# The second layer's modulation, multiplied and summed on VectorE instead of TensorE, in the weight stream of a one-core block kernel

## The reference, cut to what matters

```python
c_act, cc_act = silu(c), silu(c_ctx)                 # two vectors of 2048
for i in range(2):
    mod_l = c_act  @ ada_w[i] + ada_b[i]             # ada_w[i]: 2048 x 6144
    mod_c = cc_act @ ada_w[i] + ada_b[i]
    sh, sc, gt = split(mod, 3)                       # for latents and for context
    h = rms_norm(x, norm_gain[i]) * (1 + sc) + sh
    y = retention(h)  if i == 0 else  attention(h)   # 8 retention heads / 16 query heads
    x = x + gt * y
```

## Time and profile before

| | us |
|---|---|
| median of 3 runs | 3257.87 |
| lowest and highest | 3254.32, 3258.62 |
| the profiled execution, its own time | 3256.36 |
| its span, first to last instruction | 3255.0 |
| TensorE busy (share) | 3185.1 (98%) |
| VectorE busy (share) | 1751.4 (54%) |
| ScalarE busy (share) | 1295.1 (40%) |
| mean granted TensorE clock, share of full | 0.995 |

### The profile page before, as it was taken

The page is one execution under the profiler, slowest core; times in us unless marked ns, Lnnn a source line. Parts: engine busy times, 40 slices in busy tenths (PEclk is TensorE's granted clock), DMA queues, the critical chain, the costliest instruction groups (busy, mean ns, idle before and its releaser), DMA issues.

```text
span 3255.0 us, 48439 instructions
## 1 busy us (share of the span) xinstructions
PE 3185.1 (98%) x20536; PEld 2764.2 (85%) x20536; DVE 1751.4 (54%) x2608; ACT 1295.1 (40%) x1878; POOL 0.2 (0%) x4
## 2 busy tenths in 40 slices
PE   8999999999999999999998999999999999999998
PEld 6677777877778787777876889988999999999998
DVE  5543544435444353444436667778776665555555
ACT  4443232232232323223233645556554444444443
POOL 0000000000000000000000000000000000000000
PEclk9999999999999999999999999999999999999999
DMA  9854433233332333323234424444655545556564
GB/s 369 313 199 175 171 113 130 97 110 130 117 129 97 111 122 117 136 97 123 101 113 181 136 98 156 143 143 154 204 171 177 182 163 169 180 193 195 195 194 149
DMA packets 153927, 508.98 MB, mean 156 GB/s; under 512 B 15344, under 2 KB 35952, under 8 KB 152944
## 3 DMA queue, kind: packets, MB, share of 16 engines
q1 hardware_dynamic: 149328, 493.03, 44.1%
q10 hardware_dynamic: 4384, 12.85, 1.0%
HBM read 501.62 MB, written 4.19 MB: 155 GB/s over the span
## 4 chain that ended last, share of the span: by engine, by line
PE 89%; DVE 5%; ACT 3%; DMA 2%; issue 1%; SPq 1%; ACTq 0%; DVEq 0%
PE bank L594 28%; PE bank L596 27%; PE bank L595 27%; PE bank L656 3%; DMA raw<-stream 1%; DVE w_lo L1722 1%; ACT w_hi L1123 1%; PE bank L874 1%; ACT a_s L1431 1%; SPq L567 0%; PE bank L820 0%; PE bank L672 0%; DVE a_s L2133 0%; DVE a_numbers L2143 0%; DMA raw_h<-stream 0%
## 5 line engine op out<-in xcount | busy, mean ns | idle before, releaser
L594 PE MATMUL bank<-h_hi,w_hi 128*128 128x256 f32 (+1 forms) x4032 | 1259.5, 312 | 11.6 <-DVE w_lo L1722 6.0
L596 PE MATMUL bank<-h_hi,w_lo 128*128 128x256 f32 (+1 forms) x4032 | 1240.0, 308 | 0.0
L595 PE MATMUL bank<-h_lo,w_hi 128*128 128x256 f32 (+1 forms) x4032 | 1239.3, 307 | 0.0
L1722 DVE TENSOR_TENSOR w_lo<-raw,w_hi 128x1024 fp32r<-128x1024 f32 x729 | 882.1, 1223 | 584.0 <-ACT w_hi L1123 580.0
L1123 ACT ACTIVATE w_hi<-raw 128x1024 fp32r<-128x1024 f32 x729 | 761.9, 1058 | 914.1 <-PE bank L596 567.4
L594 PEld LDWEIGHTS bank<-h_hi,w_hi 128*128 128x128 f32 x4032 | 759.5, 188 | 84.2 <-issue 38.8
L595 PEld LDWEIGHTS bank<-h_lo,w_hi 128*128 128x128 f32 x4032 | 759.8, 188 | 44.8 <-issue 3.1
L596 PEld LDWEIGHTS bank<-h_hi,w_lo 128*128 128x128 f32 x4032 | 759.3, 188 | 43.7
L594 PE MATMUL bank<-w_hi,h_hi 128*128 128x512 f32 x704 | 286.7, 407 | 13.3 <-DVE w_lo L1722 6.5
L596 PE MATMUL bank<-w_hi,h_lo 128*128 128x512 f32 x704 | 276.5, 393 | 0.0
L595 PE MATMUL bank<-w_lo,h_hi 128*128 128x512 f32 x704 | 275.9, 392 | 0.0
(11 more groups left out here) (265 smaller groups left out, 2869.3 us busy)
## 6 DMA issues: line engine op xcount, KB each, us to landing
raw<-stream SPq DMA_DIRECT2D x904, 512.0 KB, 4.2
raw_h<-stream SPq DMA_DIRECT2D x32, 512.0 KB, 10.4
res<-tokens_in ACTq DMA_DIRECT2D x4, 1024.0 KB, 8.6
vg<-mem_in ACTq DMA_DIRECT2D x4, 512.0 KB, 8.8
h_hi<-mem_kv ACTq DMA_DIRECT2D x2, 1024.0 KB, 10.3
out<-res SPq DMA_DIRECT2D x4, 512.0 KB, 3.0
mem_kv<-qk ACTq DMA_DIRECT2D x1, 1024.0 KB, 7.9
mem_kv<-vg ACTq DMA_DIRECT2D x1, 1024.0 KB, 7.3
```

The lines of the kernel that those rows point to most:

```text
L594: pe.matmul(out, sh, mh, start=start, stop=False, **checks)
L595: pe.matmul(out, sh, ml, start=False, stop=False, **checks)
L596: return pe.matmul(out, sl, mh, start=False, stop=stop, **checks)
L1722: dve.tensor_tensor(in_quarters(m.low(raw)[:, :]), m.raw[SLOT[raw]], in_quarters(m.w_hi[slot][:, :]).bitcast(F32), ALU.subtract).then_inc( ...
```

## The change

The 96 chunks of layer 1 leave TensorE. They stay in the stream, 512 KB each, in another layout: a chunk `("mod", q, t)` now holds, for 2 x 128 of the 6144 outputs (on the partitions), the weights of a quarter `q` of the 2048 inputs. VectorE multiplies it with the condition, which has been laid across all partitions, and sums along the row: for each chunk two output tiles times two conditions, so four instructions `tensor_tensor_reduce` over 512 elements, each with a second small one behind it that writes the sum. The first quarter starts from the bias, later ones from the sum so far. This is done in VectorE's `weights_to`, just ahead of the low part of the next weight in the stream. `MODS` puts the chunks at places of heads 1 to 7: 16 in each of heads 1 to 6, less two places that are left empty at each change of the quarter, and 6 at the tiles of head 7.

The condition goes through memory: ScalarE's queue writes it once (16 KB) and SyncE's queue loads a quarter of it, the same 4 KB to all 128 partitions (512 KB), at four points of the stream (`RELOAD`), behind the last use of the quarter before. `modulated` multiplies the gain in one instruction in the last head. A raw buffer with a `mod` chunk is free when VectorE has read it. Layer 0's modulation is as it was.

```diff
-for _h in range(1, RET_HEADS - 1):
-    BESIDE[_h] = modulation_beside(places_of_head((1,) * 8, (1,) * 8), [(1, n) for n in range(3 * _h - 3, 3 * _h)])
-
-BESIDE[RET_HEADS - 1] = modulation_beside(
-    places_of_head((1,) * 6 + (0,), ()) + [(("o",), 2), (("t", 7), 0)] + [(("r", n), 2) for n in range(KT // 2)],
-    [(1, n) for n in range(18, 24)])
+for _h in range(1, RET_HEADS):
+    BESIDE[_h] = {}
+
+MOD_QUARTERS, MOD_PAIRS = 4, MOD_TILES // 2
+MOD_K = P // MOD_QUARTERS
+def modulation_on_vector():
+    steps = [(q, t) for q in range(MOD_QUARTERS) for t in range(MOD_PAIRS)]
+    out, gap = {}, 0
+    for h in range(1, RET_HEADS):
+        last = h == RET_HEADS - 1
+        places = [("t", i) for i in range(6 if last else 8)]
+        if not last:
+            places += [("v", 0), ("v", 1)] + [("r", n) for n in (0, 1, 2, 3, 5, 7)]
+        for place in places:
+            if not steps:
+                break
+            if steps[0][1] == 0 and steps[0][0] and gap < 2:
+                gap += 1
+                continue
+            gap = 0
+            out[(h, *place)] = steps.pop(0)
+    return out
...
+RELOAD = {WHERE["ada", 0, MOD_TILES // 2 - 1][3] + 12: 0}
+for _q in range(1, MOD_QUARTERS):
+    RELOAD[FIRST["mod", _q - 1, MOD_PAIRS - 1] + SLOTS] = _q
...
 # SyncE, for each chunk c of the stream
+        if c in RELOAD:
+            q = RELOAD[c]
+            if q == 0:
+                sp.wait_ge(s.load["c_out"], 16)
+                sp.wait_ge(*s["ada_turned"].at(*GROUPS[-1]))
+            else:
+                sp.wait_ge(*s["modded"].at(q - 1, MOD_PAIRS - 1))
+            rows = d["c_rows"][MOD_K * q:MOD_K * (q + 1), :].rearrange("a b -> (a b)").unsqueeze(0)
+            sp.dma_start(m.c_rows[:, :, :, :].rearrange("p a b c -> p (a b c)"), rows.broadcast_to([P, MOD_K * 2 * KT])
+                         ).then_inc(s.load["c_rows"], 16)
+        if before is not None and MOD_USE[before]:
+            sp.wait_ge(*s["modded"].at(*STREAM[before][0][1:]))
...
 # VectorE
     def weights_to(c, count=SLOTS):
         while split[0] < min(Q[c] + count, len(SPLIT)) and NEEDS[SPLIT[split[0]]] <= c:
             n, raw = split[0], SPLIT[split[0]]
             split[0] += 1
+            while mods and FIRST[mods[0]] < raw:
+                modulate(*mods.pop(0)[1:])
             dve.wait_ge(s.hi, n + 1)
...
+    def modulate(q, t):
+        c = FIRST["mod", q, t]
+        dve.wait_ge(s.raw[SLOT[c]], 16 * USE[c])
+        if t == 0:
+            dve.wait_ge(s.load["c_rows"], 16 * (q + 1))
+        if q or t:
+            dve.wait_ge(*s["modded"].now())
+        for j in range(2):
+            k = 2 * t + j
+            w = m.raw[SLOT[c]][:, 2 * j:2 * j + 2, :].rearrange("p a (b c) -> p (a b) c", c=KT)
+            for b in range(2):
+                x = m.mod[1][:, k, b:b + 1]
+                start = x if q else m.bias1[:, 1, k - KT:k - KT + 1] if KT <= k < 2 * KT else m.param("ada_b1", k, 1)
+                i = dve.tensor_tensor_reduce(out=w if b else m.products[:, j, :, :], in0=w, in1=m.c_rows[:, :, b, :], scale=1.0, scalar=start,
+                                             op0=ALU.mult, op1=ALU.add, accum_out=x)
+        i.then_inc(*s["modded"].up(q, t))
```

More of the change, by code:

```diff
@@ L161, in beside @@
             ada(layer, n, (c,))
+        if (h, *slot) in MODS:
+            q, t = MODS[(h, *slot)]
+            out.append((("mod", q, t), "ada_w", 1, MOD_K * q, 0, 2 * P * t, 0))
     beside("start", "begin")
@@ L257 @@
 RAW_USE = [b[0][0] == "ada" for b in STREAM]
-SPLIT = [c for c in range(CHUNKS) if not RAW_USE[c]]
+MOD_USE = [b[0][0] == "mod" for b in STREAM]
+SPLIT = [c for c in range(CHUNKS) if not RAW_USE[c] and not MOD_USE[c]]
 Q = [0]
-for _raw in RAW_USE:
-    Q.append(Q[-1] + (not _raw))
+for _c in range(CHUNKS):
+    Q.append(Q[-1] + (not RAW_USE[_c] and not MOD_USE[_c]))
+DONE = [_c + 1 - sum(MOD_USE[:_c + 1]) for _c in range(CHUNKS)]
 WIDEST = WHERE["mv", 1][7] // (2 * WIDE) * (2 * WIDE)
@@ L453, in __init__ @@
         self.o_rstd = sb("o_rstd", [P, T])
+        self.products = nc.alloc_sbuf_tensor_at("products", [P, 2, MOD_K, KT], BF16, offset=at[0] - 4 * T)
         self.rope0 = sb("r_rope", [P, 4, L])
@@ L562, in sync_program @@
         slot, before = SLOT[c], BEFORE[c]
-        if before is not None and RAW_USE[before]:
-            sp.wait_ge(s.mm, before + 1)
+        if c in RELOAD:
[10 more added lines that the diff above has]
+            sp.wait_ge(*s["modded"].at(*STREAM[before][0][1:]))
+        elif before is not None and RAW_USE[before]:
+            sp.wait_ge(s.mm, DONE[before])
         elif before is not None:
@@ L1129, in done @@
     def done(what, n=2):
-        act.wait_ge(s.mm, WHERE[what][n - 1] + 1)
+        act.wait_ge(s.mm, DONE[WHERE[what][n - 1]])
     def psum(*what):
@@ L1235, in scalar_program @@
                 tokens_in(n // 2 - 1)
+            if half and n == 3:
+                act.wait_ge(*s["cond_rows"].at())
+                act.dma_start(d["c_rows"], flat(m.cond_rows)).then_inc(s.load["c_out"], 16)
     for n in range(2):
@@ L1713, in vector_program @@
     split = [0]
+    mods = [("mod", q, t) for q in range(MOD_QUARTERS) for t in range(MOD_PAIRS)]
     def weights_to(c, count=SLOTS):
@@ L1728, in done @@
     def done(what, n=2):
-        dve.wait_ge(s.mm, WHERE[what][n - 1] + 1)
+        dve.wait_ge(s.mm, DONE[WHERE[what][n - 1]])
     def psum(*what):
@@ L2022, in vector_program @@
                     add_square("x1", 2 * n + j, BOTH)
-                beside(h, "r", n)
+            beside(h, "r", n)
+            if last and n == 0:
+                modulated()
     for side, cols in ((0, LAT), (1, SIDE)):
@@ L2406 @@
     stream = np.empty((CHUNKS, P, CHUNK), np.float32)
-    for c, (_, name, layer, k0, nk, n0, nn) in enumerate(STREAM):
+    for c, (what, name, layer, k0, nk, n0, nn) in enumerate(STREAM):
+        if what[0] == "mod":
+            block = w[name][layer][:, n0:n0 + 2 * P].reshape(KT, P, 2, P)[:, k0:k0 + MOD_K]
+            stream[c].reshape(P, 2, MOD_K, KT)[...] = block.transpose(3, 2, 1, 0)
+            continue
         block = w[name][layer][k0 * P:(k0 + nk) * P, n0:n0 + nn]
```

37 lines of the change are left out of this document (21 added, 16 removed).

## The result

| us | before | after |
|---|---|---|
| median (4 runs of each, on the same chip) | 3257.16 | 3171.45 |
| lowest and highest | 3254.32, 3258.62 | 3170.17, 3177.02 |
| span of the profiled execution (its own time) | 3255.0 | 3170.1 (3171.53) |

The ratio is 0.9743 (95% interval 0.973 to 0.9755): 2.6% faster. The forecast was 3171.

What follows compares the result with a forecast made beforehand. TensorE, busy for 98% of the span, was taken as the bound. Terms of 64 + 5.3 + 5.6 + 9.5 + 2.2 = 86.6 us came off 3256.4, giving 3169.8, plus 1.5 to the median: 3171 us, range 3163 to 3200.

Steps and rivals of the forecast that it cites:

- What a chunk costs TensorE in heads 1 to 6: Heads 1 to 6: 0.80 us a chunk, 10.7 us a head with the turns, 64 us (47 to 67) saved.
- The last head's output pairs: Last head: the next six output pairs go from 7.03 us each to 5.44, saving 9.5 us.
- The chain to the first pair: Last head: square root some 6 us earlier without the late DMA, so the first output pair ends 5.6 us sooner.
- now it begins with the end of the tile: Last head: tile 3's tanh starts when the tile ends, 1722.9 instead of 1727.44, and the pair ends at 1728.9.
- The two chunks behind the outputs: Last head: removing them saves nothing, since TensorE waits for the sums of squares until 1710.74 anyway.
- The start of layer 1: Start of layer 1: two low parts of 1.14 us each, made ahead of the last pair, save 2.2 us (0 to 3).
- VectorE's price: VectorE: 0.80 us an instruction with its write, 3.2 a chunk (2.4 to 5.8), 72% of a head, all hidden.
- Half rate: Rival on VectorE: a chunk costs 5.8 us, heads last 188 to 198 us, 3201 in all; 10 in 100.
- The slow load: Rival: the condition's load takes 25 us instead of 4.2, some 10 us at each of four, 3211; 4 in 100.
- The dearer instruction: Rival on VectorE: gain undone from 6.2 us a chunk on; at 2 us an instruction about 3411; 5 in 100.
- Nothing is gained: Rival: TensorE's matmul stream gets a wait at each tile in place of the chunk; 2 in 100.
- the end of the `ada` records: Sign in the profile after: TensorE's `ada` line has about half its records and ends near 340 us.

Runs made afterwards that it cites:

- b_one: The kernel before, with only one of the four matmuls of each layer-1 modulation chunk kept: 3256.64 us, ratio 0.9997.
- b_nolast: The kernel before, with head 7's 24 modulation chunks moved to heads 1 to 6, two at every tile, still on TensorE: 3240.05 us, ratio 0.995.
- a_none: The changed kernel without layer 1's modulation chunks, multiplications and condition loads, its bias standing in: 3173.16 us, ratio 0.9742 to the kernel before.
- a_nogap: The changed kernel without the two empty places at each change of quarter: 3172.08 us, ratio 0.9736 to the kernel before.
- a_twice: The changed kernel with each multiplication with its sum done twice, the extra sum unread: 3210.33 us, ratio 0.9855 to the kernel before.
- a_thrice: The changed kernel with each multiplication with its sum done three times, the extra sums unread: 3513.58 us, ratio 1.0787 to the kernel before.
- b_paired: The kernel before, with heads 1 to 6's layer-1 chunks two at a time at every second place: 3250.55 us, ratio 0.9981.

## Why the prediction was right, and where a term was off

**What a chunk costs TensorE in heads 1 to 6** held: 10.7 us a head, 0.80 a chunk by the distance of tiles. `b_one` shows that it is the break; had I priced the records (0.64) or the bare distance (0.57), I would have had 47 to 55 us instead of 64. The three stretches up to the last mean gave 69.2 of 69.3 us.

**The total** agrees better than its terms. The sum took off 86.6 us and the profiled spans differ by 84.9. These 1.7 us too many met the 1.5 us that I had added because the profiled execution before lay under its median; the one after lies 0.1 above its own. That the median came within 0.5 us is in part luck.

**The last head's output pairs** held: from 1734.51 to 1776.67 there were six pairs of 7.03 us; after, they are 5.44 apart (1666.52, 1671.96, and so on), 9.5 us for six.

**The chain to the first pair** was right in its mechanism and 1.2 us off in size. ScalarE's square root in the changed kernel, where in the kernel before a copy stood ahead of it that had waited 3.90 us for a DMA:

```profile
1643.63 0.69 ACT L1206 ACTIVATE o_rstd<-bank,eps 128x512 f32<-128x512 f32 x1 [1.97 <-PE bank L823]
```

It now waits for the mean alone. VectorE's rows of the changed kernel at the first and the last pair:

```profile
1661.08 1.66 DVE L1979 SCALAR_TENSOR_TENSOR res<-bank,mod,res 128x256 f32<-128x256 f32 x4 [0.27 <-PE bank L643]
...
1666.52 1.66 DVE L1979 SCALAR_TENSOR_TENSOR res<-bank,mod,res 128x256 f32<-128x256 f32 x4 [0.91 <-PE bank L643]
...
1699.16 1.66 DVE L2106 SCALAR_TENSOR_TENSOR res<-bank,mod,res 128x256 f32<-128x256 f32 x4 [2.38 <-PE bank L643]
...
1706.41 0.42 DVE L2127 TENSOR_TENSOR h_lo<-a_s,h_hi 128x256 fp32r<-128x256 f32 x1
```

The tanh of tile 3 starts at 1655.04 in this kernel, and the additions stand 6.04 us behind it, as forecast (6.0). But the next pair's first product comes at 1660.88, 19.3 us behind the mean, where I had 18.2 (23.77 less 5.6). The gain was 4.4. The step that was short is "now it begins with the end of the tile", where I let tile 3 take what it took before. TensorE's timeline after shows why it took longer:

```profile
1641.55 2.04 PE L823 MATMUL bank<-qk,ones_dv 128*128 128x512 f32 x2 [2.77 <-DVE qk L2046]
1642.61 1.42 PE L641 MATMUL bank<-h_hi,w_hi 128*128 128x512 f32 x1
1643.82 0.63 PE L642 MATMUL bank<-h_lo,w_hi 128*128 128x512 f32 x1
```

The mean takes 2.04 us here and 1.10 before. By stretch, the 3.3 us from the mean on, this kernel and then `b_nolast`:

```profile
1641.50:1644.80 3.30, 3.25 (x6) 2.00 (x7) 3.30 (x5) 0.85 (x2) 0.00 (x0) 0.54 0.00 0
```

```profile
1709.00:1712.30 3.30, 3.29 (x13) 2.39 (x14) 3.30 (x5) 0.82 (x2) 0.00 (x0) 1.00 0.00 0
```

Both waited the same 2.77 us for the mean. One was granted 0.54 of the clock after it, about its lower level of 1.2 GHz, the other all of it (2.4), and starts 13 records instead of 6. From the mean to the first additions the one needs 19.53 us (1641.55 to 1661.08), the other 18.10 (1709.02 to 1727.12). These 1.4 us cover the missing 1.2. The two chunks behind the outputs, of which I wrote that they "give nothing", covered part of that wait: without them it is 2.77 us and not 1.76.

Behind that same wait `a_none` was granted 0.72 over 3.3 us and needs 19.69 us to the first additions (1641.38 to 1661.07), since the lower clock begins and ends later there: 3.0 to 4.0 us behind the mean it is still 0.50, where the changed kernel has 1.00 again. `a_nogap` was granted 0.50 and needs 20.98 (1639.58 to 1660.56), 2.9 more than `b_nolast`:

```profile
1639.58:1642.88 3.30, 3.30 (x6) 1.98 (x7) 3.30 (x5) 0.81 (x2) 0.00 (x0) 0.50 0.00 0
```

The Trainium skill (TensorE: Matmul & The Clock Gate, What's actually happening) says that the point at which the clock changes varies from run to run of one kernel. The traces here are of different kernels, one execution of each, so that they fit this and do not show it.

**The start of layer 1** was 2.2 us in the forecast and 1.3 in fact, within its bounds of 0 to 3. The first `h_lo` starts 7.25 us behind the last additions (1699.16 to 1706.41) instead of 8.20 (from 1782.49): 0.95 of the 1.14 for the `w_lo` that stood in front. Of the second `w_lo` only a third of a microsecond arrives, since the chain through ScalarE paces what comes behind, as I had noted.

**VectorE's price** was a little too high: 2.7 us a chunk for 3.2, 68% of a head for 72%, 1994 us busy for 2040. `a_none` shows that all of it is hidden, and so the error cost nothing. The lower end of my range does not follow from the reasons beside it: 0.4 us more in each of six heads and 0.8 at the start of layer 1 are 3.2 us, which gives 3168 and not 3163.

**The rivals.** Half rate is refuted for this instruction: 745 ns with the sum, against 752 for the scalar-tensor-tensor without one. The Trainium skill (Vector Engine (DVE) Microarchitecture Reference, Points that are easy to get wrong) has the half rate for a scalar-tensor-tensor with two sources in SBUF that are not bf16. The profile lists the instruction used here as a custom operation with a read of the accumulator behind it, so the trace shows that the rule does not reach it, and leaves open whether it holds for a scalar-tensor-tensor with a sum. My price for it was tried in `a_twice` at 6.0 us a chunk: 3210 where I had 3201, 39 us back instead of 30. The slow load is refuted by the 4.3 us of its landing. The dearer instruction is refuted too, by the 2.7 us of a chunk; its turning point lies between 6.0 us a chunk, still 1.4% faster, and the 9.3 us of `a_thrice`, 7.9% slower. I had put it at 6.2, which no run tests closely. "Nothing is gained" falls with the list of waits.

**The signs.** One did not come: I had put the end of the `ada` records near 340 us, and the last of the 768, half of before, start at 368.5, since some of layer 0's chunks stand at head 0's output pairs, behind its mean. No term hung on it.

**What stays open.** Why low parts are late in `a_twice` while VectorE still has 7 to 13% of idle time: by dependent chains on VectorE, or because raw buffers come free later when VectorE reads them late. Both grow with the doubled work, and no run separates them. The doubled kernels also have waits between their instructions that the changed kernel has not.

## What to carry to other kernels

Price a small operation in a dense matmul stream by the distance between two undisturbed events on either side of it, and compare with the same distance where it is absent; here its records and the bare gap were both too small, and one matmul cost as much as four. Work that moves to an idle engine is free only as long as the parts it makes in between come ahead of their use: here all was hidden with that engine 68% busy, at 87% one head in three was untouched, and at 93% none. Where small work is taken out from beside a wait, look at the granted clock behind that wait as well: here it was 1.00 in the three kernels that have the two chunks there (the one before, `b_one`, `b_paired`), and lower in three of the four above that do not. That the chunks kept it is not shown.

## What the runs showed of the hardware that I had not expected

- The accumulator's read (81 ns) costs no time of its own in a row of such instructions: multiplications of 512 elements take 0.745 us and start 0.67 us apart with the read between them. With semaphores between them (`a_twice`) it is 0.72 to 0.80.
- Four matmuls into four quarters of a bank break the stream for 0.57 us, one of them for 0.55 us.
- The same 4 KB of memory, loaded to 128 partitions, landed in 4.3 us, like 512 KB of different data (4.1).
- After one and the same wait of 2.77 us TensorE was granted 1.00, 0.72, 0.54 and 0.50 of its clock over 3.3 us in four kernels; from the mean to the first additions they need 18.10, 19.69, 19.53 and 20.98 us.
